# A hybrid decoder layer: weight products woven into the delta rule, value sums woven into the prompt's attention

## What is computed

```python
h = rmsnorm(x, norm_w) @ w_in                 # qkv (1536), z (512), b, a (4+4), qb, kb, vb (512 each), two gates (1024 each)
q, k, v, g, beta = delta_prep(...)            # causal conv + SiLU, L2 norm, decays
o_a = gated_delta_chunked(q, k, v, g, beta)   # prompt; the sample uses the recurrent form with state_delta
y_a = (rmsnorm(o_a) * norm_w * silu(z)) @ w_proj_a
y_b = moba_prompt(rope(qb), rope(kb), vb) @ w_proj_b      # own block and past blocks of 256 keys
# sample: 16 pages of 128 cached keys and values per token; blocks by q.mean(k), top 3 of 8; softmax over them and the own key
hp = x + (sigmoid(gate_a) * y_a + sigmoid(gate_b) * y_b) @ w_out
hp = hp + square(relu(rmsnorm(hp) @ w_up)) @ w_down
```

## Time and profile before

| | |
|---|---|
| runs | 1203.51 us median (1201.94 to 1208.23, n = 3) |
| profiled execution | 1195.09 us, span 1193.3 us, mean granted PE clock 0.943 |
| PE busy | 1083.5 us, 91%, 8054 instructions |
| PE weight load | 1011.3 us, 85% |
| DVE / ACT / POOL busy | 643.3 (54%) / 468.3 (39%) / 255.8 us (21%) |
| DMA | 152.67 MB, mean 128 GB/s |

### The profile page before, as it was taken

One profiled execution on the slowest core, in us unless ns is written; L12 is line 12 of the kernel. 1 busy time (PEld: TensorE's weight loads), 2 busy tenths in 40 slices (PEclk: granted clock), 3 DMA queues, 4 the chain that ended last, 5 costly groups with the idle time before them and its releaser, 6 DMA issues.

```text
span 1193.3 us, 21265 instructions
## 1 busy us (share of the span) xinstructions
PE 1083.5 (91%) x8054; PEld 1011.3 (85%) x8054; DVE 643.3 (54%) x892; ACT 468.3 (39%) x707; POOL 255.8 (21%) x113
## 2 busy tenths in 40 slices
PE   6997899788987679879977999999999999999997
PEld 5997899755776569758857799999999999999997
DVE  5228887698725675685544426555433433433443
ACT  6422554424333644554534122244413413513443
POOL 0033666786400253454330000000000000000000
PEclk9998899958898899989988899999999999999999
DMA  8376777766510144645548115433333332223311
GB/s 268 108 239 187 223 204 209 212 188 175 144 44 1 53 138 136 181 129 158 151 119 217 53 49 164 133 99 89 89 89 93 98 93 88 88 88 92 100 55 72
DMA packets 179256, 152.67 MB, mean 128 GB/s; under 512 B 8913, under 2 KB 141723, under 8 KB 178918
## 3 DMA queue, kind: packets, MB, share of 16 engines
q1 hardware_dynamic: 137414, 124.72, 35.3%
q10 hardware_dynamic: 41768, 26.91, 7.8%
HBM read 142.77 MB, written 8.93 MB: 127 GB/s over the span
## 4 chain that ended last, share of the span: by engine, by line
PE 77%; DVE 11%; ACT 4%; issue 3%; POOL 2%; ACTq 1%; DMA 1%; SPq 1%; DVEq 0%; POOLq 0%
PE ps L416 56%; PE ps L1799 6%; PE ps L1786 3%; PE ps L1686 2%; PE ps L1676 2%; POOL v_low L574 2%; PE ps L1700 2%; DVE w_low L405 1%; DVE lg L1030 1%; PE ps L1543 1%; ACTq L390 1%; DVE v_low L1265 1%; ACT w_high L400 1%; ACT v_high L828 1%; PE ps L1906 1%
## 5 line engine op out<-in xcount | busy, mean ns | idle before, releaser
L400 ACT ACTIVATE w_high<-w_raw 128x1024 fp32r<-128x1024 f32 x125 | 132.3, 1059 | 431.3 <-PE ps L416 404.3
L416 PE MATMUL ps<-xh,w_high 128*128 128x256 f32 x1216 | 257.9, 294 | 12.5 <-DVE w_low L405 7.1
L405 DVE TENSOR_TENSOR w_low<-w_raw,w_high 128x1024 fp32r<-128x1024 f32 x125 | 160.5, 1285 | 195.3 <-ACT w_high L400 195.0
L416 PE MATMUL ps<-xl,w_high 128*128 128x256 f32 x1216 | 249.9, 287 | 0.0
L416 PE MATMUL ps<-xh,w_low 128*128 128x256 f32 x1216 | 249.5, 287 | 0.0
L416 PEld LDWEIGHTS ps<-xh,w_high 128*128 128x128 f32 x1216 | 193.5, 194 | 20.5 <-issue 19.7
L416 PEld LDWEIGHTS ps<-xl,w_high 128*128 128x128 f32 x1216 | 193.9, 193 | 0.0
L416 PEld LDWEIGHTS ps<-xh,w_low 128*128 128x128 f32 x1216 | 193.4, 193 | 0.0
L557 POOL TENSOR_TENSOR ring<-ring,qb 128x1024 f32<-128x1024 f32 x64 | 157.9, 2480 | 161.4 <-DMA ring<-in_cache_k 89.7
L416 PE MATMUL ps<-mh,w_high 128*128 128x256 f32 (+1 forms) x640 | 129.3, 283 | 2.4 <-issue 2.4
L416 PE MATMUL ps<-ml,w_high 128*128 128x256 f32 (+1 forms) x640 | 129.6, 284 | 0.0
(11 more groups left out here) (358 smaller groups left out, 1485.5 us busy)
## 6 DMA issues: line engine op xcount, KB each, us to landing
ring<-in_cache_k SPq DMA_DIRECT2D x128, 256.0 KB, 3.0
ring<-in_cache_v SPq DMA_DIRECT2D x128, 256.0 KB, 2.8
w_raw<-in_w_in ACTq DMA_DIRECT2D x74, 256.0 KB, 3.9
w_raw<-in_w_up SPq DMA_DIRECT2D x64, 256.0 KB, 3.1
w_raw<-in_w_down SPq DMA_DIRECT2D x64, 256.0 KB, 2.8
w_raw<-in_w_in SPq DMA_DIRECT2D x16, 256.0 KB, 7.8
w_raw<-in_w_out SPq DMA_DIRECT2D x16, 256.0 KB, 3.0
ht_dram<-ht ACTq DMA_DIRECT2D x1, 2080.0 KB, 14.1
```

The source lines that it names most:

```text
L400: act.activation(w_high[:, u % 2], w_raw[:, s], ACT.Copy).then_inc(S_hi, 1)
L405: dve.tensor_tensor(w_low[:, u % 2], w_raw[:, u % 4], w_high[:, u % 2].bitcast(F32), ALU.subtract).then_inc(S_lo, 1)
L416: last = pe.matmul(out[:, a:b], w[:, u % 2, k, :], x[:, i, a:b], start=(first + i == 0 and w is w_high and x is rhs_h), stop=(first + i == ...
```

## The change

The units get a new order, and what stands beside what is exchanged.

- `UNITS` is q (4), ba, c (12), z (4), gate_a (8), k (4), v (4), gate_b (8). Only the first 19 (up to z1) come before the delta rule.
- z2, z3 and the 8 units of gate_a are "fill": PE runs them chunk by chunk between the steps of the delta rule (`fill_to`, 80 chunks over 88 steps). All of them write into the same bank pair. ACT copies each out raw, and applies SiLU to `zs` and sigmoid to `gate_a` later in one instruction each.
- The products and reductions of the sample's keys go on through the delta rule (`keys_share`: 16 groups before, 48 in it). The query is spread to all partitions one token at a time.
- The 8 k and v units follow the delta rule, and the selection stands between them.
- The value sums stand in the steps of the prompt's attention, two groups a step, with a second pair of buffers (`v_high2`, `v_low2`). The probabilities are scaled by the inverse row sums on DVE (`scale_probs`), and PE transposes them with the identity; `dg` is gone.
- Gates 1 to 7 are no longer in the attention and the selection. Gate 8 comes after the values, as before.
- The memory map is new. SP's key loop is written out; the value loop stays a loop.

The core of the diff:

```diff
-UNITS1 = ([("q", j, C_Q + P * j) for j in range(4)] + [("ba", 0, C_BA)]
-          + [("k", j, C_K + P * j) for j in range(4)] + [("v", j, C_V + P * j) for j in range(4)]
-          + [("c", j, P * j) for j in range(12)] + [("z", j, C_Z + P * j) for j in range(4)])
-N1 = len(UNITS1)
-U_GATE = N1
+UNITS = ([("q", j, C_Q + P * j) for j in range(4)] + [("ba", 0, C_BA)] + [("c", j, P * j) for j in range(12)]
+         + [("z", j, C_Z + P * j) for j in range(4)] + [("g", j, C_GA + P * j) for j in range(8)]
+         + [("k", j, C_K + P * j) for j in range(4)] + [("v", j, C_V + P * j) for j in range(4)]
+         + [("g", 8 + j, C_GB + P * j) for j in range(8)])
+U_C, U_HEADS, N1 = 5, 8, 19
+U_FILL, U_K, U_V, U_GATE = 19, 29, 33, 29
+U_LATE = U_GATE + 8
+N_FILL = U_K - U_FILL
...
-VALUES = {"sums": 1, "decays": 1, "products": 1, "start": 1, "right": 1, "inverse_k": 1, "new_v": 1, "new_state": 1,
-          "normalise": 1, "turn_out": 1}
...
+def fill_share(i):
+
+    return min(N_FILL * KT, max(0, N_FILL * KT * (i + 1) // (len(STEPS) - 4)))
+
+
+def fills_ended(i):
+
+    return [f for f in range(N_FILL) if fill_share(i - 2) < KT * (f + 1) <= fill_share(i - 1)]
...
-    return 0 if u < 8 else 2 if u < U_C or u >= U_Z else 1 + u % 2
+    return 0 if u < 8 else 1 + u % 2
+
+
+KEYS1 = sum(keys_in_unit(u) for u in range(N1))
+
+
+def keys_share(i):
+
+    return min(GROUPS, KEYS1 + (i + 1) * 3 // 5)
...
-            return unit_ps(u % 2 if u else 3)
-
-        def gate_ps(n):
-            return unit_ps(3 if n < GATES_EARLY else (U_GATE + n) % 2)
-
-
-        def gate_share(n):
-
-            return (GATES_EARLY - 1) * KT * (n + 1) // NA
+
+            return unit_ps(3 if u == 0 else 1 if U_FILL <= u < U_K else u % 2)
+
+        def value_parts(i):
+
+            high, low = ((v_high, v_low), (v_high2, v_low2))[i // 2 % 2]
+            return high[:, i % 2], low[:, i % 2]
...
+            for i in range(0, GROUPS, 2):
+                g.wait_ge(S["v_high_out"], i + 1)
+                high, low = value_parts(i)
+                g.tensor_tensor(low, ring[:, i % 4].rearrange("p g c -> p (g c)"), high.bitcast(F32), ALU.subtract).then_inc(S["v_low_pool"], 1)
...
+            def fill(f):
+
+                u = U_FILL + f
+                kind, j, _ = UNITS[u]
+                act.wait_ge(unit_done, u + 1)
+                if kind == "g" and j == 0:
+                    act.wait_ge(ht_kept, 16)
+                A((zs if kind == "z" else gate_a)[:, j], mix_ps(u), ACT.Copy).then_inc(unit_out, 1)
+                split_high(act, u + 2)
+                if u + 5 < U_LATE:
+                    load_unit(act, u + 5)
+                if kind == "z" and j == 3:
+                    act.wait_ge(unit_out, u + 1)
+                    A(zs[:], zs[:], ACT.Silu).then_inc(*did("zs_silu"))
 
...
+            values(0, 2)
+            exponent(0)
+            exponent(1)
+            for n in range(NA):
+                q_t, h = divmod(n, HB)
+                if h == OUT_HEAD and q_t >= 1:
+                    attention_high(q_t - 1)
+                turned_probs(n)
+                if n + 2 < NA:
+                    exponent(n + 2)
+                if n + 1 < NA:
+                    values(2 * n + 2, 2)
+            attention_high(3)
...
+            act.wait_ge(S["pv_done"], GROUPS)
+            for u in range(U_LATE, U_LATE + 4):
+                load_unit(act, u)
...
-                TS(dg[:, n % 2], ident, rrs[:, n % 2:n % 2 + 1], None, ALU.mult).then_inc(S["diag_out"], 1)
...
+            def scale_probs(n):
+
+                N = (n // HB + 1) * P
+                v.wait_ge(S["att_exp"], n + 1)
+                link(v.reciprocal(rrs[:, n % 2:n % 2 + 1], rs[:, n:n + 1]))
+                TS(prob[:, n % 2, 0:N], prob[:, n % 2, 0:N], rrs[:, n % 2:n % 2 + 1], None, ALU.mult)\
+                    .then_inc(S["prob_scaled"], 1)
...
+            def fill_to(n):
+
+                for i in range(filled[0], n):
+                    f, k = divmod(i, KT)
+                    u = U_FILL + f
+                    if k == 0:
+                        pe.wait_ge(S_lo, u + 1)
+                        pe.wait_ge(unit_out, u if f else u - 1)
+                    end = product(pe, u, mix_ps(u), xh[:, k:k + 1], xl[:, k:k + 1], range(k, k + 1), whole=KT, first=k)
+                    if k == KT - 1:
+                        end.then_inc(unit_done, 1)
+                filled[0] = max(filled[0], n)
...
-                    last = mm(bank(2 + n % 2)[:, t * P:(t + 1) * P], prob[:, n % 2, t * P:(t + 1) * P], dg[:, n % 2],
-                              start=True, stop=True, skip_group_check=True)
...
+                    last = tr(bank(2 + n % 2)[:, t * P:(t + 1) * P], prob[:, n % 2, t * P:(t + 1) * P], ident)
...
+            scores(2)
+            for n in range(NA):
+                turn_probs(n)
+                if n + 3 < NA:
+                    scores(n + 3)
+                values(2 * n, 2)
+                if n >= 1:
+                    pv_prompt(n - 1)
```

More of the change, by code:

```diff
@@ L57 @@
 NCH = SEQ // CHUNK
-HIGH_AT, LOW_AT = 1, 3
+OUT_HEAD = 1
 NA = HB * SEQ // P
@@ L843, in _ @@
                 n_lv = (LEVELS - 1) * rep + lv
-                values(VALUES.get(stage.rstrip("0123456789"), 0))
-                if taken >= GROUPS and not loaded:
-                    load_last_gates()
-                    loaded = True
-                taken += VALUES.get(stage.rstrip("0123456789"), 0)
                 if stage == "decays":
@@ L1371, in _, with rows_out @@
                        ALU.subtract).then_inc(S["ona_l_out"], 1)
-                values(VALUES.get(stage.rstrip("0123456789"), 0))
-            values(GROUPS)
+                for f in fills_ended(i):
+                    split_low(v, U_FILL + f + 2)
+                lg_keys(keys_share(i))
+            for f in range(N_FILL):
+                if KT * (f + 1) > fill_share(len(STEPS) - 2):
+                    split_low(v, U_FILL + f + 2)
+            lg_keys(GROUPS)
+            def rows_out(m):
+                v.wait_ge(S["mq_turned"], m + 1)
+                v.tensor_copy(rows_kv[:, (m - 4) * P:(m - 3) * P], bank(5, P, NS)).then_inc(S["mts_out"], 1)
@@ L1651, in gate @@
-            def gate(n, first=0, last=KT):
-                u = U_GATE + n
-                if first == 0:
-                    pe.wait_ge(S_lo, u + 1)
-                    if 0 < n < GATES_EARLY:
-                        pe.wait_ge(S["gate_out"], n)
-                    elif n >= GATES_EARLY + 2:
-                        pe.wait_ge(S["gate_out"], n - 1)
-                end = product(pe, u, gate_ps(n), xh[:, first:last], xl[:, first:last], range(first, last),
-                              whole=KT, first=first)
-                if last == KT:
-                    end.then_inc(unit_done, 1)
@@ L1736, in _ @@
-            pe.wait_ge(*done("sel_red"))
-            tr(bank(6, P, NS), s1[:, 0:8], ident)
-            tr(bank(6, 2 * P, NS)[:, P:2 * P], s1[:, 8:16], ident).then_inc(*did("sel2_turned"))
-            gate(4)
-            pe.wait_ge(*done("bias_ready"))
-            for i in range(2):
-                last = mm(bank(4 + i), cf[0:NS, K_ONE:K_ONE + P], bd8[:, 4 * i:4 * i + 4, :].rearrange("r b n -> r (b n)"),
-                          start=True, stop=True)
-            last.then_inc(*did("bias_sums"))
@@ new lines, in _, with gate @@
+            scores(0)
+            scores(1)
+            scores(2)
+            for n in range(NA):
+                turn_probs(n)
[4 more added lines that the diff above has]
+                    pv_prompt(n - 1)
+            pv_prompt(NA - 1)
+            turn_values(NS - 1)
+            def gate(n, first=0, last=KT):
+                u = U_GATE + n
+                if first == 0:
+                    pe.wait_ge(S_lo, u + 1)
+                    if n >= 10:
+                        pe.wait_ge(unit_out, u - 1)
+                end = product(pe, u, mix_ps(u), xh[:, first:last], xl[:, first:last], range(first, last),
+                              whole=KT, first=first)
+                if last == KT:
+                    end.then_inc(unit_done, 1)
```

1140 lines of the change are left out of this document (574 added, 566 removed).

## The result

The changed kernel takes 1245.85 us in the median (1237.94 to 1249.47, n = 4) against 1202.72 for the kernel before on the same chip: 1.035 times its time (95% interval 1.031 to 1.040). It is slower by some 43 us; the forecast was 18 us faster. The profiled execution took 1244.34 us with a span of 1242.5.

What follows compares the result with a forecast made beforehand. It took TensorE (PE) as the bound, with time to gain from fewer instructions or idle stretches. Stage terms put gate 8 at 614.8 instead of 633.6 us, -18.8, so 1203.5 - 19 = 1184.5 us; range 1160 to 1214.

Steps and rivals of the forecast that it cites:

- SP's queue is the floor: Attention with the values: issuing four pages, 4.6 to 4.7 us, bounds each step; 4.95 us taken, 153.4 in all.
- that case: Slower rival, attention: a loop of page, high, low and slot closes over POOL; 5.9 us a step, +28 us, chance 0.20.
- steps that don't grow with the query tile: Attention, expected sign in the changed profile: steps of 4.9 to 5.0 us whatever the q tile.
- the stage's ends: Attention with the values: 10 us for the first pages' parts and the last steps, besides 29 steps.
- The argument against the rival: Attention, against the slower rival (0.20): DVE's and POOL's low parts ran side by side before, at 1.28 and 2.51 us.
- The price of a page: Value pages on SP's queue in the attention: 1.15 us to issue each, and 2.8 us until it has landed.
- The term for DVE behind POOL: Delta rule: +3 us for DVE instructions behind a POOL one, keys replacing value parts of the same size.
- The wait for the bank: Delta rule: each fill unit's first chunk waits for ACT to copy the unit before; half of ten show, +5 us.
- The even spacing: Delta rule: a level pair holds 3.64 chunks (2.6 us) instead of 2 value groups (2.0), +7.5 us over 12 pairs.
- the start of the delta rule: Forecast at 153 us, with 19 units ahead of it, not 30.
- DVE stretches the delta rule: Rival, chance 0.16: DVE's work and locks make the delta rule 228 us, steps 5.0; the gain is eaten, 1200 us.
- carried 559.7 over: From gate 8 to the end: nothing is edited after 633.6 us, so its 559.7 us were kept unchanged.

Runs made afterwards that it cites:

- e1_swap: The changed kernel with the engines of the low value parts exchanged, DVE taking the even group and POOL the odd one: 1213.98 us, ratio 1.009.
- e7_swap_order: e1_swap with ACT's two high value parts of a step also put ahead of the exponent: 1214.32 us, ratio 1.009.
- e4_keys: The changed kernel with POOL's key and query product cut to 16 of 1,024 columns for the 48 groups beside the delta rule: 1223.26 us, ratio 1.015.
- k1_keys_quiet: e1_swap with the delta rule's 48 key reductions put only beside the levels and the new values: 1205.65 us, ratio 0.999.
- f1_fill: k1_keys_quiet with the 80 fill chunks put where the kernel before had its value sums: 1199.78 us, ratio 0.997.
- p1_pad: e1_swap with 155 more instructions on PE, waits already met, between the last value sums and gate 8: 1207.97 us, ratio 1.005.
- g1_before_shift: The kernel before with 102 more instructions on PE, waits already met, before gate 8: 1218.34 us, ratio 1.013.
- f2_fill_pad: f1_fill with 60 more instructions on PE, waits already met, at the start of the attention: 1186.07 us, ratio 0.986.

## Why the prediction was wrong

*The attention's step* was the step that failed: "SP's queue is the floor", 4.95 us. It is the floor (e1_swap and e7_swap_order reach 4.9 with ACT waiting for pages), but the changed kernel never came down to it. I added up the times of a ring slot and left out that ACT's high parts stand behind the exponent, the exponent behind DVE's row maximum, and this behind a low part that can't run beside POOL's. All of it could be read from the order of the instructions and from the 1.94 us of `dg`. I gave that case 0.20 with a step of 5.9 and +28 us, as a rival; it measured 5.88 in the mean and +35.5. The prediction also named steps that don't grow with the query tile, and they grow, from 5.48 to 6.20. The 29 steps account for 27 us of the 35.5; the other 8 are the stage's ends, for which I had put 10 us and which take 18 (188.9 - 29 x 5.88), and about as much in e1_swap. The argument against the rival, that both low parts ran side by side before, overlooked that DVE's was issued there when POOL's had ended or not begun (median 1.21 us of 32). Two of those 32 did begin inside one of POOL's, at 491.39 and 596.07 us, and took 2.04 and 2.28 us, so the hold-up could be read from the trace before. In the new step ACT hands them out 1.0 us apart. The price of a page, 1.15 us, does not come out of the rows named for it (7.27 / 7 = 1.04, 2.67 / 3 = 0.89), but the runs bear it out nearly: 1.17 us between most issues, 1.22 in the mean.

*The delta rule*, forecast 213, measured 230.6. The term for DVE behind POOL was +3; e4_keys puts it at 20. I had taken keys and value parts as equal loads on POOL. POOL had 89.65 us of work in 207.2 before and 130.6 in 230.6 now, and of the four DVE lines that PE waited for longest there, three read SBUF alone (L1173 11.0 us, L1203 8.0, L1187 6.6); the fourth, L1235 (13.8), reads PSUM and itself takes 0.69 us each time. The wait for the bank was +5 forecast; the profile has 12.0 us of PE waiting for the copies of gate_a:

```profile
PE ps L439 <- ACT gate_a L753: 12.0, 5, 4.4
PE ps L1577 <- DVE sqb L1235: 13.8, 4, 5.4
PE ps L1741 <- DVE sqb L1173: 11.0, 4, 5.8
```

The even spacing (+7.5) has the right sign; k1_keys_quiet and f1_fill together took about 15 us off the first scores (454.8 against 469.9), by moving keys and chunks to other stages. How these 15 us divide between the two is open, since the start of the delta rule varied by 10 us between profiles of kernels that are the same up to there (152.2 to 162.3). The DVE work that the rival "DVE stretches the delta rule" quotes (45.77 of 59.00) is not among.

*From gate 8 to the end* I wrote that nothing is edited and carried 559.7 over. Nothing is, but the code moved, and that costs 14 us (p1_pad, g1_before_shift, f2_fill_pad); the sum had no term for it.

*What held*: the start of the delta rule (153 and 153.4, where the spread of 10 us between profiles makes so close a match luck), the selection (84 and 85.9), the gap (11.3 and 10.1), and that PE's and SP's work would allow a gain. Without the loop's 28 to 32 us and the 13 to 14 us of code placement the change would stand at about 1200 to 1205 us, no change; the gain of 1.4% needed the keys and the chunks in other places too. The rival "DVE stretches the delta rule" was right in its mechanism.

## What to carry to other kernels

When work is woven into a stage, write down each engine's order for one step and follow the loop through all of them, with who holds whom; the sum of each engine's work and of the queue is only the floor. Put a POOL instruction where DVE's next one reads PSUM (0.68 us beside POOL, L1181) or reduces one operand (1.21, L1057), and give DVE the part that is ready first. A single SBUF operand is not enough: the scaling of prob has one, and took 2.59 us. When an untouched stretch gets slower, look at the engine's idle time without a releaser and at the instruction queue before looking at data.

## What was not expected of the hardware

A loop on PE ran without fetching its code in later passes, or fetched it each time, by where its body lies. Body of 1,570 instructions, start in blocks of 256: 45.37 (before, p1_pad) and 45.00 (f2_fill_pad) had no fetches in the later passes and 558 to 560 us; 44.77 (after, e1_swap) and 45.77 (g1_before_shift) had fetches, stalls of 1 to 2.3 us at the returns, half clock at them and 573 to 574 us. That fits a limit on how many blocks the body touches, counted from a place that isn't the program's start. As an estimate: if some 27 to 58 instructions stand ahead of the program, the two slow placements touch 8 blocks and the three fast ones 7; no run here shows the limit itself.
